# Two decoder layers in one fused kernel: the layer loop written out, the norm at the layer border taken early, memory rows prepared later, the result turned and stored by quarters

## The chip, the cores and the metric

The kernel runs on one core of one Trainium2 chip. The metric is the time of one execution on the device in microseconds (us). A core has five engines that run side by side, each through its own program: TensorE (PE, matrix products; PEld is its weight load), VectorE (DVE), ScalarE (ACT), GpSimd (POOL) and SyncE (SP, which here only issues transfers). They hand work to each other over semaphores.

## The reference, cut to what matters

One inference step of a trunk of two layers for two groups: 256 prompt tokens and 8 samples of 4 new tokens. All weights are float32, the model width is 1024, the feed-forward width 2816.

```python
for l in range(DEPTH):                      # DEPTH = 2
    mk, mv = memory_kv(mem_prompt, p)       # rms(mem) @ w_ckv; keys normed per head
    hp, ... = decoder_layer(hp, ...)        # prompt tokens
    hs, ... = decoder_layer(hs, ...)        # sample tokens, with caches

def decoder_layer(x, ...):
    x = x + 0.5 * swiglu_ffn(rms_norm(x, p['ln_ffn1']), p['w_ffn1_in'], p['w_ffn1_out'])
    y, ... = mixer_groups(rms_norm(x, p['ln_mix']), ...)     # pooling | convolution | attention
    x = x + y
    x = x + memory_attend(rms_norm(x, p['ln_cross']), mk, mv, p)
    x = x + 0.5 * swiglu_ffn(rms_norm(x, p['ln_ffn2']), p['w_ffn2_in'], p['w_ffn2_out'])
    return x, ...
```

`rms_norm(x, g)` is `x * rsqrt(mean(x*x) + eps) * g`, row by row. The outputs are the two final `x` and, for each layer, keys, values and states.

## The kernel before, in words

The activations of both groups lie together in one tile `x` of 8 chunks of 128 features by T = 288 tokens. Every large product runs over **units** of weights: a unit is 256 output features by up to 1024 input features, 1 MB (`UNIT`, 128 x 2048 elements); an output projection of the feed-forward takes three units (1024, 1024 and 768 input features) for each of its four pairs of output chunks `m`. One layer has 97 units, numbered in `UNITS`. SyncE loads unit `u` into the buffer `raw[u % 2]` (`load`, L460). ScalarE rounds it to `w_hi[u % 2]`, VectorE subtracts and gets `w_lo[u % 2]` (`split`, L638 and L864), each in two halves; `release` (L384) names what ScalarE waits for before it overwrites the buffer: the product that used unit `u - 2`, and for the first two units of a layer every product of the layer before. TensorE (`unit`, L1343) multiplies with three products for each pair of chunks, high by high, low by high, high by low: 48 products of 128 x 128 by 128 x 288 for a full unit.

The norm before a product has two parts. `norm_in(L, n, m)` (L653 and L891) takes one quarter `m` of `x` (two chunks): ScalarE writes `h_hi` = x times gain, rounded, and the squares; VectorE writes `h_lo` and adds the squares up. `norm_root` (L664, L905) takes the root and reciprocal of the mean, which TensorE sums in `norm` (L1359) after the first unit of the product that follows: the first unit needs only `h_hi` and `h_lo`, the factor `norm_r` is applied to its result.

**Start.** SyncE issues the constants, x_prompt, x_sample, mem_prompt and the page numbers, then the weights (L454 to L458). TensorE turns 10 banks (L1399): four of x, one of samples, one of parameters, and, after the memory rows have been squared (ScalarE, L695 to L699) and scaled (VectorE, L967), four of memory rows into `mem_t`. VectorE copies each bank out (L966 to L983). All engines go on once `start_taken` is 10 (TensorE, GpSimd) or 6 (ScalarE).

**Layers.** Each engine runs a hardware loop `Fori(0, DEPTH) as L` around its whole layer program; the values it waits for are computed from the register L (`half_value`, `turn_value`, `passed`). At the top of the loop VectorE copies the layer's parameters from `prm_all` to `prm` (L987), then splits unit 0 and takes the four quarters of the first norm. The feed-forward's input units run in an inner loop (`pair_in`, two units each pass). In the first feed-forward (`f1out`) the next norm's quarters are taken between the splits of the output projection (L686, L956); in the second (`f2out`) they aren't, since the next norm belongs to the next pass of the loop.

**End.** After the last projection TensorE turns `x` back to rows, 24 transposes in three groups (L1759), VectorE copies each group to `y_rows` (L1326) and SyncE stores both results with two transfers (L500).

The banks M[0..3] of PSUM serve the start's and the end's transposes and, in between, the sums of the norms (`STAT`, bank 1) and attention scores.

## Time and profile before

| | us |
|---|---|
| median of 3 runs | 1662.29 |
| lowest | 1660.37 |
| highest | 2834.34 |
| span of the profiled execution | 1658.5 |

| engine | busy us | share of the span |
|---|---|---|
| TensorE | 1577.8 | 95% |
| TensorE weight loads | 1423.0 | 86% |
| VectorE | 975.1 | 59% |
| ScalarE | 594.7 | 36% |
| GpSimd | 125.9 | 8% |

The span is from the first to the last instruction on the core in the profiled execution; a run's time also holds what lies around it. Weight loads overlap products. The engines' busy times overlap each other too, so they don't add up to the span: the engine with 95% is the one whose idle stretches make up the rest. The profiler took one execution; every duration below is of that one.

### The profile page before, as it was taken

The page shows a single profiled execution, that of the slowest core. Times are in us where ns is not written, and L with a number is a line of the kernel's source. Part 1 is how long each engine was busy: PE and PEld are TensorE (multiplying, and loading weights), DVE is VectorE, ACT ScalarE, POOL GpSimd, SP SyncE. Part 2 cuts the span into 40 slices and gives each one's busy share as a digit, 9 for nine tenths or more (in the row PEclk, how much of TensorE's full clock was granted, in tenths as well). Part 3 has the DMA queues.
Part 4 walks back from the last instruction along what each step waited for, and adds up shares of the span by engine and source line. Part 5 has one row for each costly group of instructions (what it writes and reads, how often), then busy time and mean ns, then how long its engine had stood idle before and what let it go on. Part 6 is the DMA issues. An engine that isn't in the chain of part 4 may idle for free. (4 is left out here: it accounts for less than half of the span.)

```text
span 1658.5 us, 29883 instructions
## 1 busy us (share of the span) xinstructions
PE 1577.8 (95%) x10908; PEld 1423.0 (86%) x10908; DVE 975.1 (59%) x1384; ACT 594.7 (36%) x827; POOL 125.9 (8%) x168
## 2 busy tenths in 40 slices
PE   5999999799999999999989999997999999999998
PEld 4999999566967679999989999985597775999997
DVE  5766557865644437665466664678565353666643
ACT  4333344033523134343353333432343221443331
POOL 3000000702001101000000000006200001000000
PEclk7999999799999999999999999999999999999999
DMA  7565554245455537564455655442555555465542
GB/s 225 157 171 158 165 166 153 77 128 191 149 175 204 174 130 198 154 175 160 146 144 163 170 153 178 154 133 78 183 178 160 171 178 178 127 177 157 171 159 99
DMA packets 310010, 263.95 MB, mean 159 GB/s; under 512 B 7096, under 2 KB 292024, under 8 KB 309882
## 3 DMA queue, kind: packets, MB, share of 16 engines
q1 hardware_dynamic: 290242, 203.14, 40.7%
q0 software_dynamic: 13776, 48.97, 8.7%
q10 hardware_dynamic: 5896, 10.54, 2.1%
q8 instruction: 64, 1.05, 0.3%
q14 instruction: 32, 0.26, 0.1%
HBM read 254.65 MB, written 8.56 MB: 159 GB/s over the span
## 5 line engine op out<-in xcount | busy, mean ns | idle before, releaser
L1336 PE MATMUL pairs<-h_hi,w_hi 128*128 128x288 f32 x1824 | 545.1, 299 | 13.0 <-DVE h_lo L862 10.8
L1336 PE MATMUL pairs<-h_hi,w_lo 128*128 128x288 f32 x1824 | 542.7, 298 | 0.0
L1336 PE MATMUL pairs<-h_lo,w_hi 128*128 128x288 f32 x1824 | 542.6, 297 | 0.0
L859 DVE TENSOR_TENSOR w_lo<-raw_weights,w_hi 128x1024 fp32r<-128x1024 f32 (+1 forms) x388 | 450.3, 1202 | 136.6 <-ACT w_hi L636 133.6
L636 ACT ACTIVATE w_hi<-raw_weights 128x1024 fp32r<-128x1024 f32 (+1 forms) x388 | 381.6, 1032 | 292.5 <-PE pairs L1336 283.3
L1336 PEld LDWEIGHTS pairs<-h_hi,w_hi 128*128 128x128 f32 x1824 | 345.9, 190 | 18.0 <-DVE h_lo L862 11.4
L1336 PEld LDWEIGHTS pairs<-h_lo,w_hi 128*128 128x128 f32 x1824 | 346.3, 190 | 0.4
L1336 PEld LDWEIGHTS pairs<-h_hi,w_lo 128*128 128x128 f32 x1824 | 345.4, 189 | 0.0
L1336 PE MATMUL pairs<-g_hi,w_lo 128*128 128x288 f32 x704 | 208.4, 296 | 0.0
L1336 PE MATMUL pairs<-g_lo,w_hi 128*128 128x288 f32 x704 | 208.3, 296 | 0.0
L1336 PE MATMUL pairs<-g_hi,w_hi 128*128 128x288 f32 x704 | 207.8, 295 | 0.0
L678 ACT ACTIVATE gate_up<-gate_up 128x288 f32<-128x288 f32 x88 | 39.2, 445 | 330.9 <-DVE gate_up L859 330.9
L1336 PEld LDWEIGHTS pairs<-g_lo,w_hi 128*128 128x128 f32 x704 | 132.5, 188 | 0.0
L1336 PEld LDWEIGHTS pairs<-g_hi,w_hi 128*128 128x128 f32 x704 | 132.3, 188 | 0.0
L1336 PEld LDWEIGHTS pairs<-g_hi,w_lo 128*128 128x128 f32 x704 | 132.1, 188 | 0.0
L859 DVE TENSOR_TENSOR gate_up<-pairs,norm_r 128x576 f32<-128x576 f32 x88 | 66.7, 758 | 97.8 <-PE pairs L1336 96.3
L1336 PE MATMUL pairs<-y_hi,w_hi 128*128 128x288 f32 x256 | 78.2, 306 | 8.0 <-DVEq L1314 6.1
L1336 PE MATMUL pairs<-y_lo,w_hi 128*128 128x288 f32 x256 | 77.8, 304 | 0.0
L1336 PE MATMUL pairs<-y_hi,w_lo 128*128 128x288 f32 x256 | 77.7, 304 | 0.0
L1336 PE MATMUL pairs<-w_hi,y_hi 128*128 128x256 f32 x256 | 72.9, 285 | 0.3 <-DVE mk_t L1269 0.3
L1336 PE MATMUL pairs<-w_hi,y_lo 128*128 128x256 f32 x256 | 72.1, 282 | 0.0
L1336 PE MATMUL pairs<-w_lo,y_hi 128*128 128x256 f32 x256 | 72.1, 282 | 0.0
(267 smaller groups left out, 1696.9 us busy)
## 6 DMA issues: line engine op xcount, KB each, us to landing
raw_weights<-in_w_ffn_in SPq DMA_DIRECT2D x176, 512.0 KB
raw_weights<-in_w_ffn_out SPq DMA_DIRECT2D x32, 1024.0 KB
raw_weights<-in_w_in SPq DMA_DIRECT2D x18, 1024.0 KB
mem_kv<-in_cache_mem_k POOLq DMA_DIRECT2D x16, 1024.0 KB, 5.3
raw_weights<-in_w_ckv SPq DMA_DIRECT2D x16, 1024.0 KB
raw_weights<-in_w_ffn_out SPq DMA_DIRECT2D x16, 768.0 KB
raw_weights<-in_w_out SPq DMA_DIRECT2D x8, 1024.0 KB
raw_weights<-in_w_cq SPq DMA_DIRECT2D x8, 1024.0 KB
```

What stands on the lines that cost most here:

```text
L636: return act.activation(out, in_, ACT.Copy)
L678: act.activation(gate_up[:, 0, :], gate_up[:, 0, :], ACT.Silu).then_inc(silu_ready, 1)
L859: return dve.tensor_tensor(out, in0, in1, op)
L1336: return pe.matmul(out, lhsT, rhs, start=start, stop=stop, **kw)
```

## The change

Eight edits that hang together:

- The layer loop is Python's `for L in range(DEPTH)`: each layer has its own code on every engine, and what is waited for is a constant. The inner loops over feed-forward units stay.
- Parameters are read from `prm_all[:, L, ...]`; the tile `prm`, its copy and its semaphore go.
- SyncE first issues the identity alone (128 columns of the constants), x and the samples, then units 0 and 1, then the rest of the constants, the memory rows and the page numbers.
- TensorE and VectorE turn and take six banks at the start, not ten; GpSimd and TensorE go on at `start_taken` 6.
- The memory rows are squared by ScalarE after the first split of layer 0's `f1out`, scaled by VectorE after the second, turned by TensorE after unit 3 of it (`memory_turn`) and taken by VectorE after the split of unit 5 (`memory_taken`).
- In layer 0's `f2out` the quarters of layer 1's first norm are taken between the splits, as in `f1out`, and unit 0 of layer 1 is split there, ahead of the last residual add.
- In layer 1's `f2out` each quarter of the result is turned one unit after its residual add (`final_turn`), into M[0:2] or M[2:4] in turn; VectorE copies the prompt's 256 rows (`final_rows`), ScalarE the samples' 32 rows, and SyncE stores both.
- ScalarE's four copies of sample rows stand in its program after all splits of the last layer; the third and fourth `final_turn` wait for the first and second of them, since they use the same banks.

```diff
-            sp.dma_start(const[:, :], a["shape_constants"]).then_inc(const_landed, 16)
-            sp.dma_start(rows_in[:, 1, :, :], a["x_prompt"].rearrange("o (c p) d -> p (o c) d", p=P)).then_inc(x_landed, 16)
+            sp.dma_start(const[:, 0:P], a["shape_constants"][:, 0:P]).then_inc(ident_landed, 16)
+            sp.dma_start(rows_in[:, 0, :, :], a["x_prompt"].rearrange("o (c p) d -> p (o c) d", p=P)).then_inc(x_landed, 16)
             sp.dma_start(x_sample_rows, a["x_sample"].rearrange("b t d -> (b t) d")).then_inc(x_landed, 16)
-            sp.dma_start(rows_in[:, 0, :, :], a["mem_prompt"].rearrange("o (c p) d -> p (o c) d", p=P)).then_inc(mem_landed, 16)
-            sp.dma_start(pages[:, :], a["page_table"].rearrange("(o b) c -> o (b c)", o=1)).then_inc(pages_landed, 16)
...
-                with sp.Fori(0, KF // 2) as i:
+                for j in range(2):
+                    load(L, FIRST, UNITS[name] + j, v[L, j], gates=True)
+                if L == 0 and name == "f1in":
+                    sp.dma_start(const[:, P:], a["shape_constants"][:, P:]).then_inc(const_landed, 16)
+                    sp.dma_start(rows_in[:, 1, :, :], a["mem_prompt"].rearrange("o (c p) d -> p (o c) d", p=P)).then_inc(mem_landed, 16)
+                    sp.dma_start(pages[:, :], a["page_table"].rearrange("(o b) c -> o (b c)", o=1)).then_inc(pages_landed, 16)
+                with sp.Fori(1, KF // 2) as i:
                     for j in range(2):
                         load(L, i, UNITS[name] + j, v[L, i * 2 + j], gates=True)
...
-            with sp.Fori(0, DEPTH) as L:
+            for L in range(DEPTH):
...
-            sp.wait_ge(rows_ready, 3)
-            sp.dma_start(o["y_prompt"].rearrange("o (c p) d -> p (o c) d", p=P), y_rows[:, 0:2, :]).then_inc(final_landed, 16)
-            sp.dma_start(o["y_sample"].rearrange("b t d -> (b t) d"), y_rows[0:TS, 2, :]).then_inc(final_landed, 16)
-            sp.wait_ge(final_landed, 32)
+            for m in range(4):
+                s = slice(2 * m * P, 2 * (m + 1) * P)
+                sp.wait_ge(rows_ready, m + 1)
+                sp.dma_start(o["y_prompt"].rearrange("o (c p) d -> p (o c) d", p=P)[:, :, s], y_rows[:, 0:2, s]).then_inc(final_landed, 16)
+                sp.wait_ge(sample_rows_ready, m + 1)
+                sp.dma_start(o["y_sample"].rearrange("b t d -> (b t) d")[:, s], y_rows[0:TS, 2, s]).then_inc(final_landed, 16)
+            sp.wait_ge(final_landed, 128)
...
-            pool.wait_ge(start_taken, 10)
+            pool.wait_ge(start_taken, 6)
+            pool.wait_ge(const_landed, 16)
...
-                if n == 0:
-                    act.wait_ge(acc_free, passed(L, 0, -1))
+                if n == 0 and L == 0:
+                    act.wait_ge(start_taken, 6)
+                elif n == 0:
+                    act.wait_ge(acc_free, passed(L - 1, 0, TURNS["f2out"][m]))
...
+                after = (L, 1) if fout == "f1out" else (L + 1, 0)
                 for n in range(1, 12):
                     split(L, 0, u0 + n)
-                    if fout == "f1out" and n in (4, 7, 10):
-                        norm_in(L, 1, n // 3 - 1)
+                    if n == 1 and L == 0 and fout == "f1out":
+                        memory_squares()
+                    if after[0] < DEPTH and n in (4, 7, 10):
+                        norm_in(*after, n // 3 - 1)
                 if fout == "f1out":
                     split(L, 0, u0 + 12)
-                    norm_in(L, 1, 3)
-
+                elif L + 1 < DEPTH:
+                    split(L + 1, 0, 0)
+                if after[0] < DEPTH:
+                    norm_in(*after, 3)
+
+            def memory_squares():
...
+                act.wait_ge(mem_landed, 16)
+                for c in range(2):
+                    act.activation(mem_squares[:, c, :], rows_in[:, 1, c, :], ACT.Square, accum_out=sm(1 + c))
+                act.drain()
+                act.activation(sm(3, 2), sm(1, 2), ACT.Sqrt, bias=eps, scale=1.0 / D_MODEL).then_inc(mem_sq, 1)
...
+            for m in range(4):
+                act.wait_ge(final_turned, m + 1)
+                copy(y_rows[0:TS, 2, 2 * m * P:2 * (m + 1) * P], M[0:TS, 2 * (m % 2) + 1, 0:2 * P]).then_inc(sample_rows_ready, 1)
...
+                after = (L, 1) if fout == "f1out" else (L + 1, 0)
                 for m in range(4):
                     for n in range(3 * m + 1, 3 * m + 4):
                         if n < 12 or fout == "f1out":
                             split(L, 0, UNITS[fout] + n)
-                        if fout == "f1out" and m > 0 and n == 3 * m + 1:
-                            norm_in(L, 1, m - 1)
+                        elif L + 1 < DEPTH:
+                            split(L + 1, 0, 0)
+                        if m > 0 and n == 3 * m + 1:
+                            if after[0] < DEPTH:
+                                norm_in(*after, m - 1)
+                            else:
+                                final_rows(m - 1)
+                        if L == 0 and fout == "f1out" and n == 2:
+                            memory_scaled()
+                        if L == 0 and fout == "f1out" and n == 5:
+                            memory_taken()
                     residual(L, TURNS[fout][m], m, 0.5)
-                if fout == "f1out":
-                    norm_in(L, 1, 3)
+                if after[0] < DEPTH:
+                    norm_in(*after, 3)
+                else:
+                    final_rows(3)
+
+            def memory_scaled():
+
+                dve.wait_ge(mem_sq, 1)
+                dve.reciprocal(sm(3, 2), sm(3, 2))
+                dve.drain()
+                for c in range(2):
+                    dve.tensor_scalar(rows_in[:, 1, c, :], rows_in[:, 1, c, :], sm(3 + c), None, ALU.mult).then_inc(mem_norm, 1)
+
+            def memory_taken():
+
+                for n in range(4):
+                    dve.wait_ge(mem_turned, n + 1)
+                    dve.tensor_copy(mem_t[:, 2 * n:2 * n + 2, :], M[:, n, :].rearrange("p (k t) -> p k t", k=2)).then_inc(mem_taken, 1)
+
+            def final_rows(m):
+
+                dve.wait_ge(final_turned, m + 1)
+                dve.tensor_copy(y_rows[:, 0:2, 2 * m * P:2 * (m + 1) * P], M[:, 2 * (m % 2), :].rearrange("p (c d) -> p c d", c=2)
+                                ).then_inc(rows_ready, 1)
...
+                        if q == 0 and m > 0 and fout == "f2out" and L + 1 == DEPTH:
+                            final_turn(L, m - 1)
+                        if q == 0 and m == 1 and fout == "f1out" and L == 0:
+                            memory_turn()
+                if fout == "f2out" and L + 1 == DEPTH:
+                    final_turn(L, 3)
...
+            def memory_turn():
+
+                pe.wait_ge(mem_norm, 2)
+                for n in range(4):
+                    for e in range(2):
+                        for c in range(2):
+                            ins = turn(M[:, n, 256 * e + P * c:256 * e + P * c + P], rows_in[:, 1, c, (2 * n + e) * P:(2 * n + e + 1) * P])
+                    ins.then_inc(mem_turned, 1)
+
+            def final_turn(L, m):
+
+                pe.wait_ge(acc_free, passed(L, 0, TURNS["f2out"][m]))
+                if m > 1:
+                    pe.wait_ge(rows_ready, m - 1)
+                    pe.wait_ge(sample_rows_ready, m - 1)
+                for c in range(3):
+                    n = P if c < 2 else TS
+                    for e in range(2):
+                        at_e = (c % 2) * 2 * P + e * P
+                        ins = turn(M[0:n, 2 * (m % 2) + c // 2, at_e:at_e + P], x[:, 2 * m + e, c * P:c * P + n])
+                ins.then_inc(final_turned, 1)
...
-            pe.wait_ge(const_landed, 16)
+            pe.wait_ge(ident_landed, 16)
             pe.wait_ge(x_landed, 32)
 
-            for n in range(10):
+            for n in range(6):
```

## Rows read from the trace of the kernel before

**Rows 1.** Page, busy; stretches: length, PE, PEld, DVE, ACT, POOL busy, clock, DMA, GB/s.
```profile
PE 1577.8 (95%) x10908; PEld 1423.0 (86%) x10908; DVE 975.1 (59%) x1384; ACT 594.7 (36%) x827; POOL 125.9 (8%) x168
...
100.00:200.00 100.00, 100.00 (x753) 100.00 (x752) 62.49 (x84) 37.28 (x47) 0.00 (x0) 1.00 0.55 163
200.00:400.00 200.00, 184.28 (x1186) 150.66 (x1184) 132.55 (x204) 65.15 (x90) 41.05 (x48) 0.93 0.44 141
400.00:600.00 200.00, 191.77 (x1199) 148.99 (x1198) 93.84 (x140) 66.65 (x114) 11.24 (x16) 0.98 0.50 169
```

**Rows 2.** TensorE's waits: who waited for whom, us in total, times, longest.
```profile
PE pairs L1336 <- ACTq L727: 8.7, 4, 3.5
...
PE pairs L1336 <- DVEq L1314: 6.1, 2, 3.1
```

**Rows 3.** Timeline of the start: start, duration, engine, operation, idle before.
```profile
13.02 1.28 ACT L697 ACT_TABLE_LOAD   x1 [13.02 <-DMA rows_in<-in_mem_prompt]
...
14.39 0.40 DVE L978 COPY params_all<-fixed 128x232 f32<-128x232 f32 x1 [1.32 <-PE fixed L1392]
...
17.85 0.30 ACT L699 ACTIVATE small<-small 128x2 f32<-128x2 f32 x1
...
18.42 1.42 DVE L972 TENSOR_SCALAR rows_in<-rows_in,small 128x1024 f32<-128x1024 f32 x2
...
19.98 3.65 PE L1392 MATMUL fixed<-shape_consts,rows_in 128*128 128x128 f32 x16 [5.63 <-DVE rows_in L972]
...
25.05 2.36 DVE L859 TENSOR_TENSOR w_lo<-raw_weights,w_hi 128x1024 fp32r<-128x1024 f32 x2 [0.18 <-issue]
...
27.89 0.61 PE L1336 MATMUL pairs<-h_hi,w_hi 128*128 128x288 f32 x1 [4.26 <-DVE h_lo L862]
```

**Rows 4.** Transfers: queue, number, KB each, us from issue to landing.
```profile
out_y_prompt<-y_rows SPq DMA_DIRECT2D x1, 1024.0 KB, 4.2
...
out_y_sample<-y_rows SPq DMA_DIRECT2D x1, 128.0 KB, 4.1
...
out_s_conv<-sample_state POOLq DMA_DIRECT2D x2, 32.0 KB, 2.9
...
out_p_conv<-prompt_state POOLq DMA_DIRECT2D x2, 30.0 KB, 2.4
...
param_rows<-in_conv_pw_b POOLq DMA_DIRECT2D x1, 2.0 KB, 7.2
```

**Rows 5.** Timeline of the layer border, by engine.
```profile
838.74 2.00 ACT L636 ACTIVATE w_hi<-raw_weights 128x1024 fp32r<-128x1024 f32 x2 [0.98 <-PE pairs L1336]
...
841.95 0.22 DVE L987 COPY params<-params_all 128x116 f32 x1 [2.46 <-issue]
...
845.20 0.61 PE L1336 MATMUL pairs<-h_hi,w_hi 128*128 128x288 f32 x1 [6.50 <-DVE h_lo L862]
```

**Rows 6.** Stretches behind two stands of TensorE, columns as in rows 1.
```profile
845.00:848.00 3.00, 2.80 (x11) 2.80 (x12) 2.85 (x7) 3.00 (x8) 0.00 (x0) 0.50 0.50 143
848.00:851.00 3.00, 3.00 (x23) 3.00 (x23) 2.85 (x6) 2.98 (x4) 0.00 (x0) 0.96 0.75 206
...
1408.00:1411.00 3.00, 3.00 (x12) 3.00 (x13) 2.23 (x2) 0.00 (x0) 0.00 (x0) 0.51 0.00 0
```

**Rows 7.** Timeline of layer 0's first output projection.
```profile
178.99 1.58 ACT L636 ACTIVATE w_hi<-raw_weights 128x768 fp32r<-128x768 f32 x2 [3.27 <-PE pairs L1336]
...
242.99 0.76 DVE L862 SCALAR_TENSOR_TENSOR x_residual<-pairs,x_residual 128x576 f32<-128x576 f32 x1 [1.34 <-PE pairs L1336]
...
244.36 0.95 DVE L862 SCALAR_TENSOR_TENSOR h_lo<-x_residual,params,h_hi 128x288 fp32r<-128x288 f32 x2 [0.61 <-ACT h_hi L661]
```

**Rows 8.** Timeline of the end.
```profile
1648.84 1.97 PE L1392 MATMUL fixed<-shape_consts,x_residual 128*128 128x128 f32 x16 [0.85 <-DVE x_residual L862]
...
1649.97 3.58 DVE L1329 COPY y_rows<-fixed 128x1024 f32<-128x1024 f32 x3 [1.19 <-PE fixed L1392]
...
1654.02 0.46 SPq L502 DMA_DIRECT2D out_y_sample<-y_rows  x1
```

## What the change does to the time, predicted from the trace

> **What bounds the kernel now.** I read the page's busy shares first: the TensorE computes 1577.8 of 1658.5 us, 95% of the span [rows 1]. So the kernel costs its matmuls plus the 80.7 us in which TensorE stands still, and an edit is worth what it does to these two. Then the table of stretches: in the feed-forward stage (100 to 200 us) TensorE is busy for 100.00 of 100 us while VectorE works 62.49 and ScalarE 37.28; weights arrive at 163 GB/s with the DMA engines 0.55 busy. There nothing but TensorE counts. The mixer and cross-attention of layer 0 (200 to 600 us) leave 15.7 + 8.2 = 23.9 us of TensorE idle, and layer 1 about as much. Then TensorE's list of waits: the longest single releasers are h_lo, the low part of the normalised input, with 4.26 us at the start [rows 3] and 6.50 at the layer border [rows 5], and ScalarE's key copies with 8.7 us over four times [rows 2]. The timeline says where: TensorE waits 5.63 us for the scaled memory rows and starts its first real unit at 27.89 us [rows 3], and at the layer border it stands from 838.70 to 845.20 (6.50 us) [rows 5]. The third place is the tail, where the result is turned, copied and stored after the last matmul [rows 8]. The change touches just these three.
>
> **1. Start, −10.1 us.** Now: the parameters are taken at 14.39 + 0.40 = 14.79; then come memory squares, square root, reciprocal, scaling, 16 transposes (19.98, 3.65 us) and their copies, and only at 25.05 does VectorE begin the low halves of weight unit 0, which brings the first unit at 27.89, 2.84 us later [rows 3]. After the change nothing of the memory lies between: VectorE goes from the parameters to unit 0, at 14.79 + 0.15 = 14.95, and the first unit starts at 14.95 + 2.84 = 17.8. That is 27.89 − 17.8 = 10.1 us. It needs two transfers. The parameter rows are the gate already: the last of them takes 7.2 us to land [rows 4], the copy at 14.39 has waited 1.32 us for their transposes [rows 3], and the queue they come on is not touched. Weight unit 0 is now issued before the memory rows and the larger part of the constants; TensorE's first transposes wait only for identity and x. ScalarE must have the first high half by 14.9, so the unit must land by about 12.5 (table load 1.28 [rows 3], first copy 1.0 [rows 5]). SyncE's queue then carries 64 KB of identity, 1 MB of x, 128 KB of samples and this 1 MB, 2.2 MB in all, against 2.6 MB that before are in at 13.02, when the memory rows release ScalarE [rows 3]; so I take it as in time. Bounds: if the parameters come 1.4 us sooner behind the smaller packets, 11.5; if the unit lands as late as 14.6, 8.0. What is moved behind (constants, memory rows, page numbers, three issues ahead of unit 2) is needed by GpSimd's loads and by the first output projection, over 100 us later. Unit 2 queues behind 1.4 MB, and is wanted only when unit 0 is through, near 27.
>
> **2. Memory rows inside layer 0's first output projection, +2.0 us.** TensorE's 16 transposes now sit on the path: the last 16 of the kernel took 1.97 us at full clock [rows 8] (3.65 at half, [rows 3]). ScalarE adds what it does from 13.02 to 18.15, less its first table load: 3.8 us [rows 3]; before its next weight copy it now idles 3.27 [rows 7], so that copy is some 0.5 us late, and the unit it feeds is wanted 6.4 us after. VectorE adds the scaling (1.42 us, [rows 3]) and four copies of 512 columns (some 0.7 each, by the 1.2 for 1024 of [rows 8]), in two portions; it is 62% busy [rows 1]. Nobody waits behind them: cover 2 us or more each, and if it were gone the price is that 0.5 to 1 us.
>
> **3. Layer border, −4.0 us.** Now [rows 5]: ScalarE starts unit 0 at 838.74, when the last unit of layer 0 is through; VectorE adds the residual, then stands 2.46 us at the loop's end, copies the parameters at 841.95, and TensorE gets h_lo at 845.20. After: three quarters of the norm are taken during the last projection. But unit 0 of layer 1 uses the same weight buffer as the last unit of layer 0 (97 units, both even), so its split still waits for the last matmul. First high half 1.0 after 838.74, first low half 1.2 behind it (halves of 2.00 [rows 5] and 2.36 [rows 3]), two handovers of 0.1: TensorE starts at 841.2, 4.0 us earlier. The last norm quarter comes 2.3 us after the residual add starts (242.99 to 245.3, [rows 7]), here at 842.3 + 2.3 = 844.6, since VectorE ends the low halves at 842.2; TensorE reaches it after 36 matmuls of 0.133 us (23 in 3 us, [rows 6]), at 846.0. No new wait.
> The clock: in the old border TensorE works at half clock to 848 (11 matmuls in 3 us at 0.50, then 23) [rows 6]; the engine had stood 6.50 us. A stand of 3.1 us (VectorE's sequencer, [rows 2]) was also followed by 3 us at 0.51 [rows 6]. The new stand is 2.5 us. I take the nearest row, a fall, so the clock term is nil; if it stays up, another 1.4 us is saved.
>
> **4. The end, −0.1 us.** Added inside the last projection: three groups of six transposes, 3 × 0.7 = 2.1 us at 1.97/16 each. And a new wait: the third group needs bank M[0:2] back, hence the first copy of sample rows, and that copy stands in ScalarE's program behind all weight splits. It can run only when the split of the last unit is done: 0.1 + 1.58 [rows 7] + about 0.45 for the copy of 256 columns (between 0.30 for 2 columns [rows 3] and 0.79 for 768, half of [rows 7]) = 2.1 us after the tenth unit, while TensorE stands. Queued behind TensorE there: unit 11; VectorE's last rows and split, with 4 us to spare. Added 4.2 us. The tail: now from the last matmul (1648.84 − 0.85 = 1647.99, [rows 8]) to the end 1658.5 is 10.5. After: residual 0.85, six transposes 0.9, one copy of 512 columns 0.7, so SyncE starts at + 2.5; second issue 0.45 later; landing 2.9, the row of a 32 KB store (bounds 2.4, the 30 KB store, and 4.1, the 128 KB store now, [rows 4]); closing 0.35 as now: 6.2. Saved 4.3. Net −0.1; −0.6 to +1.4.
> The Trainium skill, "DMA: Bandwidth & Descriptors" (section on the anatomy of one DMA), fits 2.0 us plus bytes over 436e3 per us to a transfer (a fit made on the GpSimd path), an argument against cutting a store in pieces. It gives an estimate of 4.4 us for 1 MB, where the 4.2 us of [rows 4] agree, and 2.6 for the last quarter; by it the end would come 0.3 us sooner.
>
> **5. Straight code, −1.0 us.** Waits on computed values become constants, the parameters are read in place (two copies go), addresses are fixed. The mixers' stalls are VectorE's and ScalarE's chains, not arithmetic; no row shows their price, so I take a few hundredths of a us for each stall there. Bounds 0 and −5 (a fifth of the 46 us). A gain in the 95% does not exist: matmuls follow each other at 0.133 us in loops and outside.
>
> **Sum.** −10.1 + 2.0 − 4.0 − 0.1 − 1.0 = −13.2 us: span 1658.5 − 13.2 = 1645.3. The median of the runs shown, 1662.29, lies 3.8 above the profiled span; with the same offset, 1649.1.
>
> **Rivals.**
> A, forecast (0.68): 1649.1, own range 1645 to 1653.
> B, the mixers gain too (0.13): their stalls shrink by the bound of 5, and the clock stays up at the border: −13.2 − 4 − 1.4 gives 1644. For it: the arithmetic behind each computed wait goes. Against: TensorE idles there on [rows 2] data chains.
> C, the start gives less, or the clock falls in the end's 2.1 us stand (0.14): unit 0 late by 2.1, clock 1.4, and a mixer stall shifted by 1 to 2: 1654.
> D, slower (0.04): instruction supply. VectorE's way back at the border took 2.46 us of nothing [rows 5]. If running unrolled code costs such a gap on TensorE, at a place with no cover, five of them (12.3) use up the gain, and it is over 2% slower from 13.2 + 33 us, 19 of them. Against: layer 0's straight stretches already run code for the first time and keep TensorE at 100%. By the Trainium skill, "Advanced Engine Details and Errata" (ISA Cache), TensorE keeps 128 KB of program in lines of 256 instructions, so straight code is fetched as it goes; by that rule such gaps could come, yet stretches without a loop show none in the trace.
> E, it does nothing (0.01): the border is bound by the shared buffer anyway and the start by a late unit: 1660.
>
> **How the numbers follow.** Likeliest 1649.1. The range to hold it 8 times in 10 takes A, most of B and C: 1642 to 1656. What a measurement tells from no change is about 2%, 33 us: faster by more would need a gain 2.5 times the sum; 0.02. Slower, D at its far end: 0.03. Same 0.95.
>
> **What would show it.** First 288-column matmul near 17.8; 16 memory transposes near 190 to 200 with no idle before them; TensorE standing 2.5 us before layer 1 with "w_lo" as releaser in place of h_lo; a stand of 2.1 us on ScalarE's y_rows copy in the last projection; last matmul to end 6.2 us. Wrong if the first unit waits for weights, if a releaser other than w_lo stands at the border, or if PE's idle in the mixers changes by more than 3 us.

## The result and the profile after

The changed kernel took 1637.16 us (median of 4 executions, 1634.72 to 1639.27) against 1662.66 of the kernel before beside it: ratio 0.9849, interval 0.9835 to 0.9864. So it is 1.5% faster, within the 2% that count as the same, as forecast; but the forecast of 1649.1 us and its range of 1642 to 1656 were missed by 12 and by 5 us. One of the kernel before's four executions took 2834 us and is left out of the ratio. The profiled span fell from 1658.5 to 1632.9 us, by 25.6 where 13.2 were predicted.

The page of the changed kernel, busy times, and two lines of TensorE's list of waits (who waited for whom, us in total, times, longest):

```profile
PE 1562.1 (96%) x10908; PEld 1408.4 (86%) x10908; DVE 972.1 (60%) x1383; ACT 590.2 (36%) x828; POOL 125.9 (8%) x168
...
PE pairs L1372 <- ACTq L743: 10.9, 4, 4.9
...
PE pairs L1372 <- DVEq L1357: 5.6, 2, 2.8
```

Against [rows 1] TensorE's busy time fell by 15.7 us (1577.8 to 1562.1) with the same number of matmuls, and its idle time by 9.9 (80.7 to 70.8). The prediction looked for nearly the whole gain in the idle time. The two mixer waits answer to [rows 2]: 8.7 became 10.9, 6.1 became 5.6, so neither gave the gain.

The start of the changed kernel (timeline: start, duration, engine, line, operation, idle before and who ended it):

```profile
13.93 1.28 ACT L644 ACT_TABLE_LOAD   x1 [13.93 <-DMA raw_weights<-in_w_ffn_in]
...
14.50 0.40 DVE L1023 COPY params_all<-fixed 128x232 f32<-128x232 f32 x1 [2.17 <-PE fixed L1434]
...
15.22 2.00 ACT L644 ACTIVATE w_hi<-raw_weights 128x1024 fp32r<-128x1024 f32 x2
16.31 2.36 DVE L878 TENSOR_TENSOR w_lo<-raw_weights,w_hi 128x1024 fp32r<-128x1024 f32 x2 [1.41 <-ACT w_hi L644]
...
19.25 0.58 PE L1372 MATMUL pairs<-h_hi,w_hi 128*128 128x288 f32 x1 [4.78 <-DVE h_lo L881]
```

The first unit starts at 19.25, not at 17.8. ScalarE gets weight unit 0 at 13.93 and only then loads the table of its functions, and VectorE, with the parameters taken at 14.90, waits 1.41 us for the first high half. So it is the weights that the first unit waits for, which the prediction had named as a sign of being wrong. Against 27.89 of [rows 3] the start is 8.6 us earlier. The memory rows, 160 us later:

```profile
186.55 1.91 PE L1434 MATMUL fixed<-shape_consts,rows_in 128*128 128x128 f32 x16
```

No idle stands before them, and they take 1.91 us. The layer border:

```profile
824.67 2.00 ACT L644 ACTIVATE w_hi<-raw_weights 128x1024 fp32r<-128x1024 f32 x2 [9.52 <-PE pairs L1372]
...
827.09 0.58 PE L1372 MATMUL pairs<-h_hi,w_hi 128*128 128x288 f32 x1 [2.51 <-issue]
```

TensorE stands 2.51 us in place of the 6.50 of [rows 5]. The stretches behind the two stands (columns as in [rows 1]):

```profile
1615.00:1618.00 3.00, 3.00 (x15) 3.00 (x15) 2.43 (x3) 0.37 (x1) 0.00 (x0) 0.53 0.56 183
826.00:829.00 3.00, 1.91 (x8) 1.94 (x9) 2.79 (x3) 0.85 (x2) 0.00 (x0) 0.62 0.02 5
829.00:832.00 3.00, 3.00 (x21) 3.00 (x20) 2.36 (x4) 3.00 (x5) 0.00 (x0) 0.81 0.78 226
```

The columns with the clock read 0.53 behind the stand of 2.08 us in the last projection, and 0.62 and then 0.81 behind the border's stand of 2.51 us: for some 3 us TensorE runs at the lower of its two levels (1.2 GHz), as after the stands of [rows 6]. That is not so in each execution: in the profiles of e6, e9 and e17 (below) the clock stays at 1.00 behind the border, and by the same matmuls the border gains 5.2 us and not 4.0. The prediction had named that case, with 1.4 us for it where 1.2 were measured. The end:

```profile
1612.15 1.58 ACT L644 ACTIVATE w_hi<-raw_weights 128x768 fp32r<-128x768 f32 x2 [4.33 <-PE pairs L1372]
1613.63 0.62 ACT L644 ACTIVATE y_rows<-fixed 32x256 f32<-32x256 f32 x2
...
1614.13 0.41 PE L1434 MATMUL fixed<-shape_consts,x_residual 128*128 128x128 f32 x2 [2.08 <-ACT y_rows L644]
...
1628.50 0.88 PE L1434 MATMUL fixed<-shape_consts,x_residual 128*128 128x128 f32 x6 [0.85 <-DVE x_residual L881]
...
1630.55 0.47 SPq L509 DMA_DIRECT2D out_y_sample<-y_rows  x1
```

The predicted stand of 2.1 us is there (2.08), behind ScalarE's copy of the sample rows; from the last matmul (1627.65) to the end it is 5.2 us where [rows 8] had 10.5. The last store is issued at 1630.55, as far behind the last matmul as predicted (2.9 us); from there to the end it is 2.3 us, where 3.25 had been taken. And there is a stand that no step of the prediction had:

```profile
631.53 2.00 ACT L644 ACTIVATE w_hi<-raw_weights 128x1024 fp32r<-128x1024 f32 x2 [3.56 <-DMA raw_weights<-in_w_ffn_in]
...
633.90 0.40 PE L1372 MATMUL pairs<-h_hi,w_hi 128*128 128x288 f32 x1 [1.71 <-DVE w_lo L878]
```

**Where the 25.6 us are.** I laid the two traces over each other: the same matmul (same tiles, same count) in both, and how much earlier it starts. Start −8.7; memory rows +1.7; the stand near 632 us +1.9; border −4.0; end +0.1 (5.4 more inside the last projection, 5.3 less behind it). That is −9.0. The other 16.6 are at no single stand. Most of them grow evenly, 0.3 us in each 37 us, wherever TensorE never stands: 1.0 from 60 to 184 us, 1.1 from 700 to 835, 2.0 from 850 to 1100. One view of the kernel before and one of the changed kernel shows it, the stretch of 60 to 180 us, columns as in [rows 1]:

```profile
60.00:180.00 120.00, 120.00 (x903) 120.00 (x902) 80.03 (x112) 44.85 (x57) 0.00 (x0) 1.00 0.56 160
```

```profile
60.00:180.00 120.00, 120.00 (x910) 120.00 (x909) 78.91 (x110) 47.54 (x61) 0.00 (x0) 1.00 0.57 164
```

Both are 120 of 120 us busy at full clock, but 910 matmuls are in it and not 903. Taken over some 8,200 neighbours at full clock, a 288-column matmul is followed by the next after 133.33 ns before and 132.35 after; the 256-column matmuls of the cross-attention's keys and values after 118.7 and 114.0. There are 8352 and 768 of them: 8.2 + 3.6 = 11.8 us.

The remaining 5 us lie in the two mixer and cross-attention stages. Here are both of them together, cut at the same matmuls: in the kernel before (203 to 600 and 1030 to 1440 us), in this execution of the changed kernel (194.8 to 586.2 and 1010.7 to 1415), and in another execution of it (e5 below, 195.8 to 587.2 and 1015 to 1424). Each line gives the sum of the two stretches, then the busy time of each engine:

```profile
sum 807.00, PE 760.81 PEld 609.83 DVE 460.77 ACT 272.26 POOL 104.47; mean PE 380.40 PEld 304.91 DVE 230.38 ACT 136.13 POOL 52.23
```

```profile
sum 795.70, PE 751.30 PEld 601.03 DVE 461.30 ACT 270.93 POOL 104.56; mean PE 375.65 PEld 300.52 DVE 230.65 ACT 135.46 POOL 52.28
```

```profile
sum 800.40, PE 753.96 PEld 602.89 DVE 461.82 ACT 270.51 POOL 104.59; mean PE 376.98 PEld 301.45 DVE 230.91 ACT 135.25 POOL 52.30
```

TensorE's idle time in them is 46.2, 44.4 and 46.4 us: the mixers' waits hardly changed. The time at the lower clock in them, added up from the traces, is 55.6, 46.4 and 54.6 us. So the stages gain 11.3 us in the first execution and 6.6 in the second, and the difference is mostly the granted clock of one execution, not the change.

### The profile page after: what moved, and what is told of

Read it like the earlier page. It is cut to its first block and busy times, and to the rows that moved or that the text cites. A ratio compares the mean times of both kernels' runs of the same rounds, so it can differ in the third digit from the quotient of the medians.

```text
span 1632.9 us, 28069 instructions
## 1 busy us (share of the span) xinstructions
PE 1562.1 (96%) x10908; PEld 1408.4 (86%) x10908; DVE 972.1 (60%) x1383; ACT 590.2 (36%) x828; POOL 125.9 (8%) x168
## 5 line engine op out<-in xcount | busy, mean ns | idle before, releaser
L1372 PEld LDWEIGHTS pairs<-g_hi,w_hi 128*128 128x128 f32 x704 | 133.1, 189 | 0.0
L1372 PE MATMUL pairs<-w_lo,y_hi 128*128 128x256 f32 x256 | 70.8, 277 | 0.0
L1372 PE MATMUL pairs<-w_hi,y_lo 128*128 128x256 f32 x256 | 70.8, 277 | 0.0
```

Of the source, the lines that this page charges most:

```text
L1372: return pe.matmul(out, lhsT, rhs, start=start, stop=stop, **kw)
```

## What could do this: two theories

Theory R: straight code. TensorE's program no longer works out wait values and addresses. Theory L: the place of the tiles. The change does away with `prm`, a tile of 480 bytes per partition, and all tiles allocated behind it (h, y and g, TensorE's moving operands) move 480 bytes towards lower addresses; the weight tiles lie ahead of it and stay. By the allocator's addresses the distance from the weights to h, y and g is then 64 modulo 128 bytes; before it was 32.

All runs stand against the kernel before on the same chip; they were made in the groups e1 to e4, e5 to e8, e9 to e12, e13 and e14, and e15 to e17, and medians of different groups come from different times or chips. All differ from the kernel before by less than 2%, except that e13 and e16 reach beyond it with one end of their intervals. Spacing is the mean of the 288-column matmuls in ns, distance is that of h, y, g from the weights modulo 128.

| run | edit | median us | ratio (interval) | spacing | distance |
|---|---|---|---|---|---|
| e1 | before + 32 bytes | 1652.3 | 0.9958 (0.9942–0.9975) | 132.34 | 64 |
| e2 | before + 64 bytes | 1654.4 | 0.9964 (0.9944–0.9983) | 132.52 | 96 |
| e3 | changed + 480 bytes | 1652.8 | 0.9943 (0.9923–0.9964) | 133.33 | 32 |
| e4 | before, layer loops written out | 1655.7 | 0.9969 (0.9957–0.9982) | 133.33 | 32 |
| e5 | changed | 1636.5 | 0.985 (0.982–0.988) | 132.27 | 64 |
| e6 | changed, late copies and table | 1634.4 | 0.983 (0.9802–0.9859) | 132.32 | 64 |
| e7 | changed, all tiles + 32 bytes | 1633.6 | 0.9844 (0.9806–0.9881) | 132.36 | 64 |
| e8 | changed, h and g at 0, y at 96 | 1641.5 | 0.9885 (0.9851–0.9919) | 132.75 | 0, 96 |
| e9 | changed, GpSimd's loads spread | 1633.1 | 0.9842 (0.9809–0.9874) | 132.30 | 64 |
| e10 | changed, low halves elsewhere | 1642.9 | 0.9879 (0.9852–0.9905) | 132.49 | mixed |
| e11 | changed, old border | 1639.8 | 0.9863 (0.984–0.9887) | 132.38 | 64 |
| e12 | changed, old end | 1637.6 | 0.9854 (0.9831–0.9877) | 132.37 | 64 |
| e13 | changed, three edits | 1633.2 | 0.9818 (0.9789–0.9846) | 132.44 | 64 |
| e14 | e13, low weights + 32 bytes | 1636.1 | 0.9835 (0.9812–0.9859) | 132.79 | 64, 32 |
| e15 | changed | 1633.4 | 0.9838 (0.9813–0.9863) | 132.43 | 64 |
| e16 | three edits | 1630.9 | 0.9816 (0.9788–0.9845) | 132.42 | 64 |
| e17 | changed + 480 bytes | 1651.8 | 0.9945 (0.9929–0.9962) | 133.33 | 32 |

## The place of the tiles against straight code

**e1 and e2: the old kernel, moved.** The edit is one unused tile behind `prm`:

```diff
         prm = sb("params", [N_PROWS])
+        sb("layout_pad", [8])
         ck_gain = sb("ck_gain", [MDH])
```

([16] in e2.) Expected of e1:

> The kernel before with one unused tile of 32 bytes behind the parameters, so that every tile from ck_gain on lies 32 bytes further; nothing else. Theory L (the faster steady rhythm of TensorE after the change, 0.1322 instead of 0.1333 us from matmul to matmul, comes from where the activations lie, since the tile prm of 480 bytes is gone and shifted all that follows by an odd multiple of 32): steady spacing 0.1322, time 10 to 13 us shorter. Theory R (the rhythm comes from straight code, whose waits need no register arithmetic): spacing 0.1333, time as before within 2 us.

Expected of e2:

> The kernel before with an unused tile of 64 bytes in the same place. Theory L in its narrow form (what counts is the place within 64 bytes): spacing 0.1333, time as before within 2 us. If any shift changes the time, the form is wider. Theory R: as before as well.

**e3: the changed kernel with the bytes put back.**

```diff
+        sb("layout_pad", [N_PROWS])
         ck_gain = sb("ck_gain", [MDH])
```

> The changed kernel with an unused tile of 480 bytes where prm lay, so that all later tiles lie where they lay before the change. Theory L: spacing back at 0.1333, 10 to 13 us slower than the changed kernel, so about 13 us (1649) faster than before. Theory R: as the changed kernel, 25 us faster than before.

**e4: only the loops written out**, on all five engines.

```diff
-            with pe.Fori(0, DEPTH) as L:
+            for L in range(DEPTH):
```

> The kernel before with the five layer loops written out and nothing else; prm and its copy stay, so the layout is that of before. Theory L: 1 to 4 us faster (VectorE's 2.5 us at the loop's end go, which shortens the border), spacing 0.1333. Theory R: 12 to 16 us faster, spacing 0.1322.

Measured, stretch of 60 to 180 us, first e1, then e3, then e4:

```profile
60.00:180.00 120.00, 120.00 (x910) 120.00 (x909) 81.11 (x112) 44.99 (x57) 0.00 (x0) 1.00 0.57 164
```

```profile
60.00:180.00 120.00, 120.00 (x902) 120.00 (x902) 78.73 (x110) 47.51 (x61) 0.00 (x0) 1.00 0.57 164
```

```profile
60.00:180.00 120.00, 120.00 (x902) 120.00 (x902) 80.11 (x111) 44.18 (x57) 0.00 (x0) 1.00 0.57 160
```

The old code with 32 bytes more runs at the changed kernel's 910, and even pair by pair its spacings are the changed kernel's (h_lo by w_hi 133.64 and 133.64, h_hi by w_lo 132.01 and 131.97). The changed code with its 480 bytes back is at 902, and so is the old code with straight loops. Theory R falls for the spacing, theory L stands. In e2 a part of it falls: 64 bytes were to change nothing, and gave 132.52. So it does not go by 64 bytes; another place in the 128 is another rate. The same layout gave means between 132.27 and 132.44 in different executions, so that 132.52 by itself says little; but e2's single pairs differ by far more (h_lo by w_hi 131.77, not 133.6), and its 256-column matmuls follow each other at 117.3 ns, not 114.0.

The times were forecast less well than the spacings. e1 is 8.8 us below the kernel before, where 10 to 13 had been expected; e3 is 8.3 below it, not 13; e4 is 5.4 below it, not 1 to 4.

**e7: is it the address or the distance?** 32 bytes ahead of the very first tile move the weights too.

```diff
+        front_pad = sb("front_pad", [8])
         raw = sb("raw_weights", [2, UNIT])
```

> The changed kernel with 32 bytes put in front of the first tile, so that the weights move by the same 32 bytes as h, y and g (all operands keep their distances). Offsets modulo 128: weights 32, h, y and g 96. Theory L-absolute (only the address of the moving operand counts): the spacing is that of the kernel before with 64 bytes more, h_hi w_lo 132.7, h_lo w_hi 131.8, h_hi w_hi 133.2, mean 132.5 ns. Theory L-relative (the distance between weights and moving operand counts): as the changed kernel, 132.0, 133.6, 131.4, mean 132.35 ns. A mean of 133.3 ns fits neither: then the weights' own address counts too.

The spacings are the changed kernel's (131.97, 133.66, 131.38; mean 132.36), not those of e2, whose h has the same own address modulo 128. The distance between weights and moving operand counts.

**e8 and e10: tiles by themselves.** In e8 64, 96 and 32 bytes are put ahead of h, y and g; in e10 `h_lo`, `y_lo`, `g_lo` are moved by 32, 96 and 64 bytes against their high halves.

```diff
+        region(16)
         h_at = region(2 * KD * T)
...
+        region(24)
         y_at = region(2 * KD * T)
...
+        region(8)
         arena = region(2 * KF * T)
```

```diff
-        h_lo = at("h_lo", [KD, T], F32R, h_at + 4 * KD * T)
+        h_lo = at("h_lo", [KD, T], F32R, h_at + 4 * KD * T + 32)
```

> The changed kernel with three tiles shifted by different amounts: offsets modulo 128 are 0 for h, 96 for y, 0 for g (weights 0). Theory L (each tile's own place sets its matmuls' spacing, with a period of 128 bytes or less): y as at 96 in the padded kernel before (mean 132.5), h and g equal to each other, at a value no run has shown: between 131.5 and 133.4 ns. If all three still go alike, it is not the place of the moving tile but something common, such as the code or the refresh of a buffer.

> The changed kernel with the low halves moved against the high halves. Offsets against the weights modulo 128, high and low: h 64 and 96, y 96 and 64, g 64 and 0. If each matmul's spacing goes by the place of its own moving operand, h_hi stays at 131.4 (w_hi) and 132.0 (w_lo) and h_lo comes to 131.8, mean 131.7 ns and 3 to 4 us less for h; y_hi comes to 133.2 and 132.7 with y_lo at 133.6; g_lo to 132.4. Rival: the spacing goes by a sequence of operands, its neighbours count, and no such sum comes out.

In e8 h and g, both at distance 0, go alike (high by low weights, high by high, low by high: h 133.20, 132.78 and 132.32; g 133.25, 132.65 and 132.46 ns), and y at 96 differs (132.55, 132.97 and 132.04): each tile's own place counts. In e10 the sum by single pairs fails: h_hi by w_hi, whose two tiles did not move, went from 131.4 to 133.1 when h_lo moved, and g_lo came to 134.35 and not 132.4. In three executions of the changed kernel itself that pair read 131.43, 130.97 and 131.78, so 133.1 is outside what one layout shows. A matmul's spacing depends on its neighbours too.

**e14: the low weights alone.**

```diff
+        region(8)
         w_lo = sb("w_lo", [2, UNIT], F32R)
+        region(24)
```

> The kernel of the three edits with the low halves of the weights alone moved by 32 bytes; w_hi, h, y and g keep their places modulo 128 (0 and 64), w_lo lies at 32. If the distance of the pair that is multiplied counts, h_hi w_lo goes from 132.0 to what a distance of 32 showed (133.6), and the two with w_hi stay at 131.4 and 133.7: mean 132.9 ns, 5 us slower in all. If what counts is the load of the next weights during a matmul, the one that runs while w_lo is loaded changes, that is h_lo w_hi (133.7), and h_hi w_lo stays at 132.0. If only the high weights count, nothing changes.

| pair | changed, ns | e14, ns |
|---|---|---|
| h_hi by w_hi | 131.42 | 133.86 |
| h_lo by w_hi | 133.64 | 131.17 |
| h_hi by w_lo | 131.97 | 133.35 |

All three changed, so none of the three rules that I had set up holds alone: the pair rule has only the third right, the rule of the next load only that h_lo by w_hi changes. The mean (132.79) came close to the first rule's 132.9 for the wrong reasons. In time e14 is 2.9 us above e13, not 5. What stays open is the rule; what is shown is the table by distance: 32 is slowest (133.33 in all four profiles), 64 fastest (132.27 to 132.44), 96 (132.52, one run) and 0 (132.8, h and g of e8) between. With 32-byte steps there are no others as long as all tiles move together. Why the distance counts at all no run shows.

The Trainium skill, "TensorE: Matmul & The Clock Gate" (section "Wait — 56ns, not 53.3ns?"), gives back-to-back matmuls at the full clock the columns over 2.4 GHz plus about 2.5 ns, with nothing about addresses or about a weight load ahead of each matmul. For 288 columns that would be an estimate of 122.5 ns; no run here came below 130.8 for any pair, and the rest moved by up to 3 ns with the place alone.

**How much of the time is it?** e15 and e17 ran side by side.

> The changed kernel itself again, beside the kernel before on the same chip, so that the versions with moved tiles can be read against it. Theory L (the place of the operand tiles costs 1 ns in each of the 288-column matmuls, the other edits are worth what the padded version showed, ratio 0.9943): ratio 0.985 to 0.988, mean spacing of the 288-column matmuls 132.3 ns again. Theory C (most of the difference seen at first was a difference of chips or of the day): ratio 0.990 to 0.995, as the padded version.

> The changed kernel again, as the measure for the two beside it: ratio 0.985.

> The changed kernel with 480 bytes in the place of the tile that it does without. By the spacings (8352 matmuls of 288 columns by 1.0 ns, 768 of 256 columns by 4.8 ns) the place is worth 8.4 + 3.7 = 12 us: 12 us more than the changed kernel beside it, and 12 to 13 less than the kernel before. Rival: the place is worth more than the spacings say (15 us, as two ratios from different chips gave), and the edits less than 10.

1651.8 against 1633.4 is 18 us, more than the 12 of the spacings. A part of the rest is the clock. Over 161 executions of the kernels here (without one whose recorded clock of 0.929 does not fit its time), an execution of the same kernel is 0.8 us longer for each 0.001 that its mean granted clock is lower, and the changed kernel has a mean of 0.981 (11 executions) where the padded one has 0.978 (16) and the kernel before 0.976 (65). Carried to 0.980 by that slope, they take 1637.2, 1649.5 and 1658.4 us: the place is worth 12.3, as its spacings say, give or take 1.5 by the scatter, and all other edits 8.9. Why the clock is higher in the faster layout was not tried. In the kernel before the same 12 us of spacing gave e1 only 8.0 us at equal clock. Where the other 4 went is not shown; in the two profiled executions, from 60 us on, TensorE worked 62.7 us at the lower clock in e1 and 55.5 before, and half of that difference is 3.6 us, but that is one execution each.

## The steps of the prediction, undone one by one

**e11: the old border.** The split of layer 1's unit 0 and its norm stand behind the last residual again.

```diff
-                    if after[0] < DEPTH and n in (4, 7, 10):
+                    if fout == "f1out" and n in (4, 7, 10):
                         norm_in(*after, n // 3 - 1)
...
-                elif L + 1 < DEPTH:
-                    split(L + 1, 0, 0)
```

> The changed kernel with the layer border as before: the split of layer 1's first weight unit and all four quarters of its norm stand behind the last residual, not inside the last projection. The step of the prediction (-4.0 us) and the trace (TensorE stands 2.51 us): TensorE stands 6.0 to 6.6 less VectorE's 2.5 us at the loop's end, so about 4.1 us, as in the version in which only the loops were written out (4.12 us); the time rises by 1.6 us and the border's gain is 2.4 of straight code and 1.6 of the earlier norm. Rival: the norm itself is worth the whole 4 us, and TensorE stands 6.5 us again.

First the first matmul of layer 1 in e4, then in e11:

```profile
844.01 0.37 PE L1336 MATMUL pairs<-h_hi,w_hi 128*128 128x288 f32 x1 [4.12 <-DVE h_lo L862]
```

```profile
833.49 0.58 PE L1365 MATMUL pairs<-h_hi,w_hi 128*128 128x288 f32 x1 [4.12 <-DVE h_lo L877]
```

4.12 us in both. The border's 6.50 us are 2.4 for VectorE's way back to the loop's start (in e4 its 2.46 us without a releaser, [rows 5], are gone) and 1.6 for the norm's place; the 2.5 that remain are put down to the shared weight buffer by the order of the program, no run parts them. By the same matmuls, e11 gains 1.3 us across the border where the changed kernel gains 4.0, since its clock stays low for 6.8 us behind the longer stand where the changed kernel has 3.4. The median is 3.3 us above e5 and 6.4 above e15, more than the 1.6 expected, but on other chips.

**e12: the old end**, 24 column blocks turned and two stores behind the last matmul.

```diff
-                        if q == 0 and m > 0 and fout == "f2out" and L + 1 == DEPTH:
-                            final_turn(L, m - 1)
```

> The changed kernel with the end of the kernel before: 32 column blocks turned after the last matmul, two stores. The prediction held the new end to be worth 0.1 us. By the trace of the changed kernel: inside the last projection 2.1 us of stand, 2.1 us of transposes and about 1.5 us of lower clock go; from the last matmul to the end 10.5 us come in place of 5.3. So the time stays the same to 0.7 us. Rival: the parts of the end do not cancel, and the difference is 2 us or more in either direction.

```profile
1626.40 1.96 PE L1435 MATMUL fixed<-shape_consts,x_residual 128*128 128x128 f32 x16 [0.85 <-DVE x_residual L875]
1628.81 1.05 PE L1435 MATMUL fixed<-shape_consts,x_residual 128*32 128x128 f32 x8 [0.44 <-DVE y_rows L986]
```

1637.6 against 1636.5 and 1633.4: no difference that the intervals tell. Against the trace of before, its last projection gains 0.6 us where e5's loses 3.7, and the tail takes 10.6 where e5's takes 5.2: what the quarters save behind the last matmul is mostly paid in front of it.

**e6: the two waits that the trace shows.** One copy to load ScalarE's table while it waits, and the sample copies between the splits:

```diff
             act.wait_ge(fills_done, 5)
+            act.activation(sm(90), eps, ACT.Copy)
...
+                    if after[0] == DEPTH and n in (5, 8, 11):
+                        sample_rows(n // 3 - 1)
```

> Two edits to the changed kernel that take away two waits its trace shows: ScalarE's copies of the sample rows stand between its weight splits and not behind them, and ScalarE loads its function table on an idle copy of one value before the first weight unit lands. If the stand of 2.08 us in the last projection waits only for that copy's place in the program, it is gone and the clock stays up there: 2.1 us, or 3.6 with the clock. If the first unit waits for the table load of 1.28 us behind the landing at 13.93 us, it starts at 17.9 to 18.0 us in place of 19.25. Together 3.4 to 4.9 us less than the changed kernel. Rival: VectorE's parameter copy at 14.5 us and the new copies between the splits make new waits, and less than 1.5 us is left of it.

```profile
4.58 1.28 ACT L725 ACT_TABLE_LOAD   x1 [4.58 <-issue]
...
14.44 2.00 ACT L644 ACTIVATE w_hi<-raw_weights 128x1024 fp32r<-128x1024 f32 x2 [8.35 <-DMA raw_weights<-in_w_ffn_in]
...
18.46 0.58 PE L1378 MATMUL pairs<-h_hi,w_hi 128*128 128x288 f32 x1 [4.56 <-DVE h_lo L887]
```

The table load is out of the way; weights landed 0.5 us later here, so the first unit starts 0.8 earlier than in the profile of the changed kernel. The Trainium skill, "ScalarE: Activation LUTs" (section "Table sets: the hidden batching unit"), says that cheap functions such as copy are in every table set; here the load at 4.58 came with the early copy, and ScalarE's splits and squares up to 20 us needed no other. In the last projection TensorE no longer stands, and the clock does not fall there, as it did in two of the three profiles of the changed kernel. The median is 1634.4, 2.1 below e5, less than the 3.4 to 4.9 expected and within the scatter of both.

**e9: the stand near 632 us.** GpSimd's loads for layer 1 wait for later pairs of the second feed-forward block.

```diff
+                def spread(i):
+                    if L > 0:
+                        pool.wait_ge(acc_ready, passed(L - 1, i, TURNS["f2in"][1]))
+                spread(1)
```

(and `spread(3)`, `spread(5)`, `spread(7)` ahead of the states and the two loads of pages.)

> The changed kernel; GpSimd issues its loads for layer 1 (1.9 MB) not all at once at about 620 to 625 us but in four portions behind the 2nd, 4th, 6th and 8th pair of the second feed-forward block. Theory P (in straight code those loads come to lie on one weight transfer, whose lateness is the new stand of TensorE near 632 us, 1.7 to 2.4 us, with a fall of the clock in some runs): the stand is gone, 1.5 to 4 us less at that place of the trace than in the changed kernel. Rival: the weights are late there for another reason, and the stand stays; or it only moves to the next portions.

Stretch of 632 to 640 us, first e5, then e9:

```profile
632.00:640.00 8.00, 5.59 (x31) 5.35 (x30) 5.57 (x8) 4.35 (x5) 0.00 (x0) 0.79 0.51 143
```

```profile
632.00:640.00 8.00, 8.00 (x63) 8.00 (x62) 5.06 (x8) 2.87 (x5) 0.75 (x2) 1.00 0.58 160
```

The stand of 2.41 us and its clock are gone, 4.2 us at this place by the same matmuls. e4 has the stand as well, and its ScalarE waits 4.75 us for weights:

```profile
643.75 2.00 ACT L636 ACTIVATE w_hi<-raw_weights 128x1024 fp32r<-128x1024 f32 x2 [4.75 <-DMA raw_weights<-in_w_ffn_in]
```

So writing out the loops brings it (e1 and e2, which keep them, have no such stand): GpSimd issues the pages 1.4 us earlier against TensorE than in the kernel before, they take 9.3 us to land where they took 6.5, and one weight transfer is late with them. In e9 the four portions are issued at 639, 664, 691 and 717 us, all later than before, and no stand is left. That the loads bring the stand is shown by e9; that just these 1.4 us do is argued. In the profiles of the versions with written-out loops and unspread loads the stand costs 1.2 to 4.6 us, by the same matmuls. By medians e9 is at 1633.1, inside the scatter of the changed kernel.

**e13 and e16: all three edits together.**

> The changed kernel with all three edits: sample copies between the weight splits, the function table loaded early, GpSimd's loads for layer 1 in four portions. If the places are independent, the gains seen one by one add: 0.8 to 1.3 us at the start, 4.2 near 640 us, 3.6 in the last projection (stand 2.1, clock 1.5): about 8 us less than the changed kernel's 1636.5, so 1627 to 1630. Rival: the order of ScalarE's work couples them, or a stall in the mixers takes part of it back: 1631 to 1634, as each alone.

> The kernel of the three edits again. If the traces are right: 6 to 8 us less than the changed kernel beside it. If the medians so far are: 3 us.

1633.2 and 1630.9 us, ratios 0.9818 and 0.9816: the first is above the 1627 to 1630 that had been added up. The profiled spans are 1629.7 and 1630.6 against 1637.8 and 1637.3 of the changed kernel, 7 us, but only 2 to 3 against its first profile, 1632.9; the medians differ by 2.5 to 3.3, and at equal clock the 11 executions of each differ by 4.7, give or take 1.8. The gain at the three places adds up in the traces; how much reaches the median lies between 2.5 and 7, and these runs don't narrow it.

## Why the prediction was wrong, point by point

1. **Start, predicted −10.1, measured −8.7.** That nothing of the memory rows lies between any more was right. The gate was not: I let the parameters gate the first unit and took the weights as in time, by 12.5 us. They came at 13.93, inside the bound of 14.6, with ScalarE's table load behind them, and the first unit waited for them. That is the sign "wrong if the first unit waits for weights"; it cost 1.4 us.
2. **Memory rows, +2.0, measured +1.7** (1.91 of transposes, no idle). Right.
3. **Border, −4.0, measured −4.0**; the stand 2.5, measured 2.51; the clock fell as taken in this execution, and stayed up in three others. The split into 2.4 of loop end and 1.6 of norm comes from e4 and e11. The releaser was shown as "issue" in place of w_lo; the name of the sign was wrong, not the step.
4. **End, −0.1, measured +0.1**, with the stand of 2.1 us at 2.08. One part was missing: the clock fell behind it (about 1.5 us); the tail, 5.2 in place of 6.2, paid most of it, since the last store was through after 2.3 us and not 3.25. The upper bound of +1.4 does not come out of its terms: 4.1 in place of 2.9 for the landing gives +1.1. So the sum came out right by two errors that cancel.
5. **Straight code, −1.0, bounds 0 and −5.** The 5 was called a fifth of the 46 us; it is a ninth. TensorE's idle time in the mixers fell by 1.8 us in one execution of the changed kernel and rose by 0.2 in another, so the sign of 3 us stayed away. e4's trace is 3.4 us ahead when layer 0's mixers are through, but there too the idle time did not fall (24.0 to 25.9 us), the time at the lower clock did (35.1 to 23.9): no gain of straight code is shown there. It then loses 4.6 at a stand that I had no term for. The cover that I had named in step 1 ("needed by GpSimd's loads and by the first output projection, over 100 us later") was about transfers; I did not ask which transfers would come earlier for the same reason.
6. **The step that failed** is the sentence "A gain in the 95% does not exist: matmuls follow each other at 0.133 us in loops and outside". It tested one cause, loops, and shut out all others. The diff takes a tile away; that was read as two copies saved, not as a move of all that lies behind it. The 11.8 us of closer matmuls, and some 3 us of clock with them, are the miss.

The sum of the steps for everything but the place of the tiles was −13.2; the padded version, which is just that, measured −8.8 by medians (1660.6 to 1651.8) and −8.9 at equal clock. With the start at −8.7 and a stand near 632 us of 1.6 to 4.4 us (e17 and e3), −13.2 becomes −7.4 to −10.2. That is 1651.8 us (1652.8 in e3), inside the range: had the bytes not moved, it would have held, with a likeliest value 3 us too low. Two misses of opposite sign met, 4 us too much from the edits and 15 us not foreseen. Rival B's 1644 was nearest, by luck: its mechanism, mixer stalls shrinking by 5 us and a clock that stays up at the border, did not happen. In rival C both pieces (less at the start, a clock fall at the end's stand) happened, but did not decide. For rival D nothing was found: in the changed kernel TensorE is busy for 180.00 of 180 us (640 to 820) and 160.00 of 160 (850 to 1010), with the output projections in them, whose units are written out one by one.

## What to carry to other kernels

When a diff adds or removes a tile, write down the addresses of the tiles behind it before and after: here 32 bytes of padding in the old kernel, with no other edit, were worth 9 us (8.8 by medians, 8.0 at equal clock), and the distance between weights and moving operand had four values to try. Compare the count of matmuls in a stretch where TensorE is 100% busy, not its busy share, which was 120.00 of 120 us in both kernels. And when code is made to run ahead, look at which transfers it issues earlier, not only at which waits it drops.

## What the hardware showed that I had not expected

The spacing of 288-column matmuls lay between 132.3 and 133.3 ns on average by the distance between the weight tiles and the moving tiles modulo 128 bytes, single pairs from 130.8 to 134.4; that of 256-column ones, in which the weights are the moving operand, moved more, from 114.0 (distance 64) to 118.7 (32). VectorE's return to the start of the layer loop cost 2.4 us with nothing else to do. And the mean granted clock of a whole execution, 0.970 to 0.987 here, goes with 0.8 us for each 0.001: it differs from one execution to the next of the same kernel by more than some of the edits are worth.
